# Cutting the weights of a two-block transformer at a later tick: where ScalarE's rounding and VectorE's subtraction stand among the side steps

## The reference

```python
def hybrid_layer(x, ...):
    h = rmsnorm(x, norm_mix)
    proj = h @ w_in
    o_a = fox_attention(to_heads(q_a, FOX_HEADS), to_heads(k_a, FOX_HEADS), to_heads(v_a, FOX_HEADS), log_f)
    ...
    o_c, o_s, o_w = nsa_attention(q_n, kc, vc, ks, vs, kw, vw)
    o_n = g[..., 0:1] * o_c + g[..., 1:2] * o_s + g[..., 2:3] * o_w
    mixed = jax.nn.sigmoid(gate_a) * y_a + jax.nn.sigmoid(gate_b) * y_b
    x = x + mixed @ w_out
    return x + jnp.square(jax.nn.relu(h @ w_up)) @ w_down
```

## Time and profile before

| | |
|---|---|
| median of 3 runs | 2779.88 us |
| lowest and highest | 2779.82 and 2782.42 us |
| the profiled execution: its time | 2780.02 us |
| its span, first to last instruction | 2777.8 us |
| mean granted clock of TensorE | 0.996 |
| instructions | 34501 |

### The profile page before, as it was taken

The page is one execution under the profiler, slowest core; times in us unless marked ns, Lnnn a source line. Parts: engine busy times, 40 slices in busy tenths (PEclk is TensorE's granted clock), DMA queues, the critical chain, the costliest instruction groups (busy, mean ns, idle before and its releaser), DMA issues.

```text
span 2777.8 us, 34501 instructions
## 1 busy us (share of the span) xinstructions
PE 2699.2 (97%) x13369; PEld 2224.2 (80%) x13369; DVE 1516.5 (55%) x2682; ACT 1141.2 (41%) x2058; POOL 205.6 (7%) x314
## 2 busy tenths in 40 slices
PE   7999999999999999999899999999999899999997
PEld 6778888887788888778778888888778788888886
DVE  6756444467564444576765653343667666643433
ACT  4644222246442222455654442232465644342331
POOL 5200000002000000021121000000020211000000
PEclk9999999999999999999999999999999999999999
DMA  4113332331132333332212233333323111322332
GB/s 128 50 35 99 99 99 93 97 90 46 35 103 95 99 99 97 97 84 78 87 43 60 92 93 97 99 99 95 104 65 106 59 49 61 104 93 93 98 99 76
DMA packets 187637, 235.58 MB, mean 85 GB/s; under 512 B 12130, under 2 KB 140612, under 8 KB 187476
## 3 DMA queue, kind: packets, MB, share of 16 engines
q1 hardware_dynamic: 184500, 225.95, 26.5%
q0 software_dynamic: 2256, 5.52, 1.0%
q10 hardware_dynamic: 720, 1.92, 0.2%
HBM read 227.05 MB, written 2.11 MB: 82 GB/s over the span
## 4 chain that ended last, share of the span: by engine, by line
PE 82%; DVE 10%; ACT 4%; issue 3%; POOL 0%; DMA 0%; ACTq 0%; DVEq 0%
PE bank L651 24%; PE bank L653 23%; PE bank L652 23%; DVE Wl L2216 2%; ACT Wh L1481 2%; PE bank L911 1%; PE bank L856 1%; PE bank L932 1%; PE bank L974 1%; PE bank L1174 1%; PE bank L975 1%; PE bank L933 1%; DVE STT L2530 1%; PE bank L841 1%; PE bank L1375 1%
## 5 line engine op out<-in xcount | busy, mean ns | idle before, releaser
L2216 DVE TENSOR_TENSOR Wl<-RAW,Wh 128x1024 fp32r<-128x1024 f32 (+3 forms) x434 | 510.5, 1199 | 396.2 <-ACT Wh L1481 395.5
L1481 ACT ACTIVATE Wh<-RAW 128x1024 fp32r<-128x1024 f32 (+3 forms) x434 | 437.8, 1032 | 406.8 <-PE bank L653 404.8
L651 PE MATMUL bank<-Hh,Wh 128*128 128x512 f32 (+1 forms) x1120 | 453.2, 405 | 2.2 <-issue 1.1
L653 PE MATMUL bank<-Hh,Wl 128*128 128x512 f32 (+1 forms) x1120 | 438.1, 391 | 0.0
L652 PE MATMUL bank<-Hl,Wh 128*128 128x512 f32 (+1 forms) x1120 | 437.3, 390 | 0.0
L651 PE MATMUL bank<-HA,Wh 128*128 128x512 f32 x704 | 274.2, 390 | 0.0
L653 PE MATMUL bank<-HA,Wl 128*128 128x512 f32 x704 | 273.9, 389 | 0.0
L652 PE MATMUL bank<-HA,Wh 128*128 128x512 f32 x704 | 273.9, 389 | 0.0
L653 PEld LDWEIGHTS bank<-Hh,Wl 128*128 128x128 f32 (+1 forms) x1120 | 209.0, 187 | 46.9
L651 PEld LDWEIGHTS bank<-Hh,Wh 128*128 128x128 f32 (+1 forms) x1120 | 209.8, 187 | 44.3 <-issue 3.9
L652 PEld LDWEIGHTS bank<-Hl,Wh 128*128 128x128 f32 (+1 forms) x1120 | 209.7, 187 | 36.9
(11 more groups left out here) (405 smaller groups left out, 4714.4 us busy)
## 6 DMA issues: line engine op xcount, KB each, us to landing
RAW<-in_w_up_dram SPq DMA_DIRECT2D x108, 512.0 KB, 3.7
RAW<-in_w_down_dram SPq DMA_DIRECT2D x108, 512.0 KB, 3.8
RAW<-in_w_in_dram SPq DMA_DIRECT2D x90, 512.0 KB, 3.6
RAW<-in_w_gate_dram SPq DMA_DIRECT2D x44, 512.0 KB, 3.6
RAW<-in_w_out_dram SPq DMA_DIRECT2D x28, 512.0 KB, 3.8
RAW<-in_cmp_w_dram SPq DMA_DIRECT2D x16, 512.0 KB, 4.0
RAW<-in_w_o_fox_dram SPq DMA_DIRECT2D x8, 512.0 KB, 4.0
RAW<-in_w_o_nsa_dram SPq DMA_DIRECT2D x8, 512.0 KB, 3.5
```

The lines of the kernel that those rows point to most:

```text
L651: pe.matmul(o, sh, mh, start=first, stop=False)
L653: return pe.matmul(o, sl, mh, start=False, stop=last)
L1481: sc.activation(M.Wh[:, v % NHL, 0:n], M.RAW[:, v % NRAW, 0:n], ACT.Copy).then_inc(G.w_hi, 1)
L2216: ve.tensor_tensor(M.Wl[:, v % NRAW, 0:n], M.RAW[:, v % NRAW, 0:n], M.Wh[:, v % NHL, 0:n].bitcast(F32), ALU.subtract).then_inc(G.w_lo, 1)
```

## The change

At the start of unit u, `next_unit()` on ScalarE and VectorE makes sure that units up to u + 1 are cut, which they normally are by then, and sets a countdown for unit u + 2. A local `tick()` takes the place of the sides' own: it advances the sides and then counts. ScalarE issues the rounding of unit u + 2 behind the side steps of the first tick of unit u, and VectorE the subtraction behind those of the second tick. In `lin_t` VectorE's second tick comes behind the evacuation of the unit's first bank, where there is one. `drain` uses the sides' own tick and doesn't count. If a unit has fewer ticks, the cut is made at the start of the next unit. Which unit is cut, the buffers and the semaphores are the same; TensorE's, GpSimd's and SP's programs are not touched.

```diff
 def scalar_program(sc, M, G, K, plan, a):
     sides = Sides()
-    tick, begin, drain = sides.tick, sides.begin, sides.drain
+    begin, drain = sides.begin, sides.drain
-    cut, unit = [0], [0]
+    cut, unit, late = [0], [0], [0, 0]
...
-    def next_unit():
-        u = unit[0]
-        unit[0] += 1
-        while cut[0] <= min(u + AHEAD, len(plan) - 1):
+    def cut_to(limit):
+        while cut[0] <= min(limit, len(plan) - 1):
             v = cut[0]
             cut[0] += 1
...
             sc.activation(M.Wh[:, v % NHL, 0:n], M.RAW[:, v % NRAW, 0:n], ACT.Copy).then_inc(G.w_hi, 1)
+    def next_unit():
+        u = unit[0]
+        unit[0] += 1
+        cut_to(u + AHEAD - 1)
+        late[:] = [1, u + AHEAD]
         return unit_of(plan, u)[0]
+
+    def tick():
+        sides.tick()
+        late[0] -= 1
+        if late[0] == 0:
+            cut_to(late[1])
```

More of the change, by code:

```diff
@@ L2217, in next_unit, with tick @@
                              ALU.subtract).then_inc(G.w_lo, 1)
-        return unit_of(plan, u)[0]
+    def next_unit():
+        u = unit[0]
+        unit[0] += 1
+        cut_to(u + AHEAD - 1)
+        late[:] = [2, u + AHEAD]
+        return unit_of(plan, u)[0]
+    def tick():
+        sides.tick()
+        late[0] -= 1
+        if late[0] == 0:
+            cut_to(late[1])
     def lin_t_units(name, kt, evac, before=None, nj=2, often=2):
```

## The result

The changed kernel took 2787.63 us (median of 11 runs, 2786.92 to 2788.85), the kernel before 2780.00 us in runs beside it. The ratio is 1.0024, with a 95% interval of 1.0016 to 1.0033. The change makes the kernel 7.6 us slower, where 12 us less was forecast. The profiled execution has a span of 2785.2 us, 7.4 us more than before, and a mean granted clock of 0.992 against 0.996.

What follows compares the result with a forecast made beforehand. TensorE, busy 2699.2 of 2777.8 us, was taken as the bound, so only its waits could be gained. Gains of 25.6 us less losses of 13.5 gave -12.1, from 2780.0 to 2768 us; own range 2759 to 2774, overall 2753 to 2784.

Steps and rivals of the forecast that it cites:

- the gains: All TensorE waits expected to shrink, at start, attentions and output, with the granted clock: 25.6 us together.
- Window attention: Six waits at L841 and L1160, with the pair in front of the score steps: 7.0 of 7.3 us gained.
- the forget and sparse attention with the clock: Waits at L911 and L932, 14 of 24.1 us gained, plus 3.0 us from the granted clock.
- the start: Unit 3's subtraction moves behind the copy TensorE waits for at L1001: 1.0 us gained.
- The output: Two waits for lower parts, in the loop over w_o_nsa, lose their cause: 0.6 us gained.
- each late subtraction: Subtractions delayed at units 11 to 13, forget keys, sparse start and wide feed-forward: 4.0, 3.6, up to 3.5, 2.3 us.
- the wide starts: First wide feed-forward units: subtraction follows the first bank's evacuation, 2.3 us late, twice, 4.5 us lost with nothing to swallow it.
- the netting of the losses: Later waits swallow delays at units 11 to 13, forget keys and sparse start, leaving losses of 6.4, 0.4 and 0.8 us.
- the clock: After a 2.1 us attention wait the granted clock falls; shorter waits should keep it, gaining 3.0 of 3.4 us.
- the rival of the waits that only move: Attention waits reappear one or two ticks on, only 8 of 24 us go, clock still falls: 2778 us, chance 0.20.
- the gated starts: First gate units, priced with the last key and value units by bank evacuation: 0.7 us a layer, 1.4 us lost together.
- weights late behind VectorE's long steps: Four stages plus half the smaller places lose 28.2 us unswallowed, against gains of 12: 2796 us, chance 0.12.

Runs made afterwards that it cites:

- e10: Late cut kept only in window, forget (from units 190, 317) and sparse attention, the w_o_nsa loop and first six units; 2750.07 us, 0.9885 of the kernel before.
- e6: The changed kernel, but units cut beside the forget-gate steps and the selected keys' lower parts cut as before the change; 2774.42 us, 0.9976 of the kernel before.
- e9: The changed kernel plus 64 zero-adding matmuls on TensorE ahead of units 13 and 103; 2786.02 us, 1.0016 of the kernel before.
- e5: The changed kernel, but with cuts at the starts of units 10, 11, 100 and 101 made as before the change; 2778.62 us, 0.9990 of the kernel before.
- e11: The changed kernel plus zero-adding matmuls on TensorE, 90 ahead of unit 13 and 64 ahead of unit 103; 2785.15 us, 1.0012 of the kernel before.
- e2: The changed kernel with ScalarE's rounding back at the unit's start, VectorE's subtraction still behind the second tick; 2783.74 us, 1.0012 of the kernel before.

## Why the prediction was wrong

**Right: what stands behind the waits, and the gains.** The prediction read from the timeline that the pair stood in front of the softmax steps, which holds, though the step that TensorE waited for was a reciprocal (above). It took 25.6 us for the gains. Had alone, in e10, they come to 30.3 us. Window attention was forecast at 7.0 us and gave 8.3, the forget and sparse attention with the clock 17.0 and 17.4, the start 1.0 and 2.6, some 1.6 of it by a fall of the clock at 30 us that the prediction had not counted. The output was forecast at 0.6 and gave 2.0, and there its having the right sign was luck: of the four waits for lower parts that the term was read from, none is in the loop over w_o_nsa. They are at units 13 (0.64 us), 211 and 338 (0.44 each) and 364 (0.15), and the first three grew. What the output gained came at units 231 (0.5 us) and 236 to 237 (0.4) of each layer.

**Right: each late subtraction, as a raw delay.** The places were named, and the delays without what was set against them too: forecast 4.0, 3.6, up to 3.5 and 2.3 us; measured as waits 5.5 and 4.0, then 3.4, 3.1 and 2.1. At the wide starts, where nothing was set against it, the term came out: forecast 4.5 us, in the ledger 4.8. That VectorE's steps run in the order issued is also what the Trainium skill says of VectorE (page "PSUM — Partial Sum Buffer", section "Engine vs sequencer instructions": strict FIFO); the timeline at 91.29 to 96 us agrees, with the subtraction starting at 94.04, when the steps in front of it are done.

**Wrong: the netting of the losses.** The step that failed is in the part on losses: "Later waits of up to 1.77 us [...] shrink by that much, since VectorE's steps get ahead", "again waits at L911 follow closely and swallow it", and "less the 0.7 us wait at L1174 soon after that vanishes". The first two take waits of the softmax chain as cover for a loss. Of these 24.1 us 14 had already been booked as gains, and the netting wants 13.0 more (7.2 and 7.0, less the 1.2 kept), out of 10.1 that were left. The pair leaves the softmax chain whether or not the weights are late, so those waits vanish anyway, and hardly anything is left to swallow a delay. e6 shows it: with the late weights undone, forget and sparse attention keep their gains, and 16.5 us come back where the prediction's netting leaves 1.2. The wait at L1174 stayed at 0.7 us twice. (Its 4.0 less 0.7 is also 3.3 and not 3.2, which changes little.) At these three places the forecast has 7.6 us net and the ledger +28.8 (12.2 + 8.8 + 7.8).

**Wrong: the clock.** It was a gain of 3.0 us in the sum. Two of the three falls before were counted, to vanish, and the places with new waits were given no price, except in the rival of the waits that only move. There are nine falls after. Where two kernels differ by a fall alone, it costs some 1.6 us; the five behind the late weights of these three places are part of the 28.8 us above.

**Missed in size:** the gated starts, +3.3 and +1.8 us with one fall of the clock, where 0.7 a layer was taken for two places together. There VectorE evacuates and squares nearly without a pause, so a subtraction put among those steps, and the wait for its rounding, delay the sum of squares at L786. The prediction priced the place by an evacuation of a feed-forward bank, which doesn't show that.

**Which rival it was.** The slower one, "weights late behind VectorE's long steps": its mechanism and its places are the ones found. Its 2796 us was too high because both of its halves were too small, the gains more so: it has 12 us of gains and 28.2 of losses, and the ledger 31.2 and 38.7. The difference of these is the 7.5 us of the table. The prediction's own marker, a sum for L651 on Wl over 30 us, was passed at 31.1.

What stays open: why the same wait brings the clock down in one kernel and not in another (below), and what ScalarE's half would do alone.

## What to carry to other kernels

When an instruction is moved back so that others run sooner, price the gain and the loss at each place by itself, and set a wait against a loss only if it would still be there once the gain is booked. Then use the move only where it gains: the same edit was 0.24% slower everywhere and 1.15% faster in the attention units alone. Where a consumer stands at a margin of nothing, as in the earlier trace rows, any long step put in front of its input can be paid in full, and a wait of some microseconds on TensorE should be given the price of a fall of the clock too.

## What the runs showed of the hardware

Most falls of the granted clock cost the same. At stretches that no edit touched, the ledgers of two kernels differ by steps of 1.53 to 1.62 us where one shows a fall and the other none. Where the clock stays down longer, it costs more: at unit 189 in e9 it is 0.50 from 1194 to 1198 us and still 0.57 in the next 2 us, and that stage costs 2.8 us more than in the changed kernel, where the same wait of 3.4 us leaves the clock at 1.00.

And the falls are not tied to the wait alone. At the start of the second wide feed-forward part TensorE stands still some 2 us for the same lower part in the changed kernel, e5, e6 and e11; the clock fell there in those three and stayed up in the changed kernel. The executions of one kernel differ in this too: the eleven of e2 took 2780.2 to 2786.9 us, with mean granted clocks from 0.995 down to 0.991. So a count of falls from one profile is one draw, and a forecast can price a fall but not place it.
